# Folding three more adaLN chunks on VectorE in an attention and MLP trunk, with the double steps of two units placed differently

## The reference, cut to what matters

```python
c_act = jax.nn.silu(c)
for i in range(DEPTH):                       # DEPTH = 2
    mod = c_act @ ada_w[i] + ada_b[i]        # ada_w[i]: 2048 x 12288
    sh_mix, sc_mix, g_mix, sh_mlp, sc_mlp, g_mlp = jnp.split(mod, N_MOD, axis=-1)
    h = rmsnorm(x, norm_mix[i]) * (1 + sc_mix) + sh_mix
    mix = fox_mixer(h, ...) if i % 2 == 0 else short_conv_mixer(h, ...)
    x = x + g_mix * mix
    h = rmsnorm(x, norm_mlp[i]) * (1 + sc_mlp) + sh_mlp
    x = x + g_mlp * (jnp.square(jax.nn.relu(h @ w_up[i])) @ w_down[i])
return rmsnorm(x, final_norm)
```

## Time and profile before

| | |
|---|---|
| time, median of 3 runs | 2293.26 us (2293.22 to 2294.5) |
| profiled execution, its own time | 2293.36 us |
| its span | 2291.5 us |
| PE busy | 2251.9 us, 98% |
| DVE busy | 1698.0 us, 74% |
| ACT busy | 1096.8 us, 48% |
| granted PE clock, mean | 0.997 |

### The profile page before, as it was taken

The page is one execution under the profiler, slowest core; times in us unless marked ns, Lnnn a source line. Parts: engine busy times, 40 slices in busy tenths (PEclk is TensorE's granted clock), DMA queues, the critical chain, the costliest instruction groups (busy, mean ns, idle before and its releaser), DMA issues.

```text
span 2291.5 us, 30019 instructions
## 1 busy us (share of the span) xinstructions
PE 2251.9 (98%) x11688; PEld 1919.4 (84%) x11688; DVE 1698.0 (74%) x1642; ACT 1096.8 (48%) x1264; POOL 173.1 (8%) x339
## 2 busy tenths in 40 slices
PE   6999999999999999999999999999999999999998
PEld 5999998878888888888878888887888888888886
DVE  6888999968958957967977888866895555555555
ACT  4355444464445435435545444446443543543553
POOL 0001221101101101101100111100110000000000
PEclk9999999999999999999999999999999999999999
DMA  9987999959968968967966888855986556565563
GB/s 363 386 320 256 347 352 368 349 191 320 340 212 304 348 212 291 336 234 274 328 243 242 305 327 331 319 184 173 320 302 215 184 184 202 184 197 188 184 214 116
DMA packets 271812, 615.71 MB, mean 269 GB/s; under 512 B 15472, under 2 KB 15808, under 8 KB 271296
## 3 DMA queue, kind: packets, MB, share of 16 engines
q1 hardware_dynamic: 220480, 437.56, 55.5%
q0 software_dynamic: 46080, 167.79, 20.1%
q10 hardware_dynamic: 5120, 8.49, 1.1%
HBM read 611.66 MB, written 2.13 MB: 268 GB/s over the span
## 4 chain that ended last, share of the span: by engine, by line
PE 90%; DVE 4%; DMA 2%; issue 2%; ACT 1%; SPq 0%; ACTq 0%; DVEq 0%
PE ps L516 19%; PE ps L517 18%; PE ps L518 18%; PE ps L504 15%; PE ps L505 8%; PE ps L491 2%; PE ps L492 2%; PE ps L493 2%; DMA start_ring<-in_ada_w_dram 2%; DVE hb L1464 1%; DVE acc L1464 1%; DVE square_out L1464 1%; DVE w_lo L1444 0%; PE ps L596 0%; ACT w_hi L916 0%
## 5 line engine op out<-in xcount | busy, mean ns | idle before, releaser
L916 ACT ACTIVATE w_hi<-raw 128x1024 fp32r<-128x1024 f32 x721 | 762.8, 1060 | 965.3 <-PE ps L518 698.3
L1444 DVE TENSOR_TENSOR w_lo<-raw,w_hi 128x1024 fp32r<-128x1024 f32 x721 | 877.3, 1223 | 443.2 <-ACT w_hi L916 441.9
L504 PE MATMUL ps<-h,w_hi 128*128 128x512 f32 x1536 | 541.2, 397 | 0.0
L516 PE MATMUL ps<-w_hi,mid 128*128 128x512 f32 x1280 | 499.8, 390 | 0.2 <-DVE w_lo L1444 0.2
L518 PE MATMUL ps<-w_lo,mid 128*128 128x512 f32 x1280 | 498.2, 389 | 0.0
L517 PE MATMUL ps<-w_hi,mid 128*128 128x512 f32 x1280 | 498.1, 389 | 0.0
L505 PE MATMUL ps<-h,w_lo 128*128 128x256 f32 x1536 | 431.2, 281 | 0.0
L504 PEld LDWEIGHTS ps<-h,w_hi 128*128 128x128 f32 x1536 | 288.4, 188 | 70.5
L516 PE MATMUL ps<-w_hi,h 128*128 128x512 f32 x756 | 298.9, 395 | 4.1 <-DVE w_lo L1444 1.9
L518 PE MATMUL ps<-w_lo,h 128*128 128x512 f32 x756 | 294.6, 390 | 0.0
L517 PE MATMUL ps<-w_hi,h 128*128 128x512 f32 x756 | 294.4, 389 | 0.0
(11 more groups left out here) (246 smaller groups left out, 1801.7 us busy)
## 6 DMA issues: line engine op xcount, KB each, us to landing
ada_raw<-in_ada_w_dram POOLq DMA_DIRECT2D x320, 512.0 KB, 6.4
raw<-in_mlp_w_up_dram SPq DMA_DIRECT2D x128, 1024.0 KB, 5.3
raw<-in_mlp_w_down_dram SPq DMA_DIRECT2D x128, 1024.0 KB, 5.6
raw<-in_fox_w_in_dram SPq DMA_DIRECT2D x48, 1024.0 KB, 11.1
raw<-in_conv_w_in_dram SPq DMA_DIRECT2D x48, 1024.0 KB, 7.5
start_ring<-in_ada_w_dram SPq DMA_DIRECT2D x64, 512.0 KB, 12.1
raw<-in_fox_w_out_dram SPq DMA_DIRECT2D x16, 1024.0 KB, 9.0
raw<-in_conv_w_out_dram SPq DMA_DIRECT2D x16, 1024.0 KB, 5.2
```

The costliest lines, as they stand in the source:

```text
L504: mm(o, hi[:, jc], both, start=(k == 0), stop=False, skip_group_check=True)
L516: mm(o, xh, hi, start=(k == first), stop=False)
L916: op(w_hi[:, e % WR], raw[:, e // 2, EK * (e % 2):EK * (e % 2 + 1)], ACT.Copy).then_inc(hi_ready, 1)
L1444: v.tensor_tensor(w_lo[:, e % WR], raw[:, e // 2, EK * (e % 2):EK * (e % 2 + 1)], w_hi[:, e % WR].bitcast(F32), ALU.subtract).then_inc(spl ...
```

## The change

It has two parts. Chunks 0, 1 and 2 are folded as well (chunk 5 stays as it is). And units 6 and 7 have step tables of their own: both still take 11 steps, but unit 6 takes single steps behind its first three pairs and double steps behind pairs 3, 4 and 6, and unit 7 takes double steps behind pairs 0, 2, 4 and 5 and none behind pair 7.

```diff
-FOLDED = [i for i, (b, _) in enumerate(ADA) if PARTS[b] in GATE or i >= A_MLP0]
+FOLDED = [i for i in range(len(ADA)) if i != A_MLP0 - 1]
...
 ELEVEN = [2, 1, 2, 1, 1, 2, 1, 1]
+RISING = [1, 1, 1, 2, 2, 1, 2, 1]
+FALLING = [2, 1, 2, 1, 2, 2, 1, 0]
...
-PLAN_QKV = plan([NONE] * N_START + [ELEVEN] * 7 + [LATE, DENSE, SEVEN, NONE])
+PLAN_QKV = plan([NONE] * N_START + [ELEVEN, RISING, FALLING] + [ELEVEN] * 4 + [LATE, DENSE, SEVEN, NONE])
```

## The result

| | before | changed |
|---|---|---|
| median | 2293.88 us (4 runs, 2293.22 to 2296.01) | 2308.10 us (4 runs, 2307.72 to 2309.35) |
| ratio | | 1.0063 [1.0051, 1.0075] |
| profiled execution, its span | 2293.36, 2291.5 us | 2307.72, 2305.7 us |
| granted PE clock, mean | 0.997 | 0.994 |

The changed kernel is 14.2 us slower: the sign that was forecast, twice its size (+7.6 us), and outside the range.

The account below looks back on a forecast made before the run. DVE was taken to bound units 6 to 11, making PE wait: 2293.4 + 6.0 (lateness) + 1.6 (lower clock) = 2301.0 us, 0.33% slower. Range 2291 to 2306 us, the main case's own 2297.5 to 2306 us.

Parts of the forecast that it names:

- What bounds the kernel: Units 6 to 9: DVE decides when PE starts the scores of groups 2 and 3; margin at group 2 0.40 us.
- What DVE is given, unit 6 and unit 7: DVE gets 9.1 us more work; reciprocals 1.1 us late, unit 7 adds 3.4 us, scores of group 2 4.1 us later.
- the second sum of unit 6: DVE's work in unit 6 from the split near 245.1 us to the reciprocals at 256.2 us, summed to 11.1 us.
- The saving of chunk 0: PE's 1.57 us from folding chunk 0, forecast to be lost in the wait before the turn of group 1.
- What PE is spared: Folded sums cost PE 0.22 us instead of 1.79 us: 1.57 us spared for a chunk, 4.7 us for three.
- Units 8 to 11: DVE gets 3.6 us more, 1.7 us covered by idle time; scores of group 3 late by 4.1 + 1.9 = 6.0 us.
- The clock: PE's clock falls behind one of two waits, at the scores of groups 2 and 3: 1.6 us, ends 0 and 3.2.
- The rule's reading that both places pay: By the Trainium skill's rule the clock falls behind both waits, making the sum +9.2 us rather than +7.6 us.
- What would show it: Signs: PE waits at groups 1 to 3, DVE windows 97% or more from 253 to 361 us, constant distance from group 3's exponentials.
- DVE has the time and PE keeps its 4.7 us: Rival: the 0.4 us margin holds 3.4 us of new DVE work, giving 2288.7 us; chance 0.12.
- The small-wait case: Rival: 3.0 us wait at the scores of group 2, clock holds, +1 to +4.5 us, about 2296 us; chance 0.16.
- The rival of a longer fall: Clock falls at both places or for longer: 6.0 + 3.2 us or more, 2303 to 2306 us; a third of 0.72.

Follow-up runs that it names:

- e1_fold_only: Kernel before with chunks 0, 1 and 2 folded and its old step tables kept: 2308.48 us, ratio 1.0062.
- e4_fold1_behind: Changed kernel with new tables for units 7 and 8, so that chunk 1 is folded behind `low_attn` of group 1: 2301.95 us, 6.15 us under the changed kernel.
- e6_tables_c: Kernel before with only chunks 0 and 1 folded as well, and its own step tables for units 6 to 12: 2290.72 us, ratio 0.9989.
- e5_tables_a: Kernel before with chunks 0, 1 and 2 folded and new step tables for units 6 to 12, chunk 1's fold behind `low_attn`: 2290.38 us, ratio 0.9987.
- e3_keep_busy: Changed kernel with unused matmuls put into PE's three long waits: 2301.95 us, ratio 1.0031 to the kernel before.
- e2_table_only: Kernel before with the new step tables of units 6 and 7, chunks 0 to 2 not folded: 2296.16 us, ratio 1.0012.
- e8_chunk2_unfolded: Changed kernel, tables included, with chunk 2 not folded: 2305.09 us, 3.0 us under the changed kernel.

## Why the prediction was right in sign and wrong in size

**What bounds the kernel: right.** DVE decides at the scores of groups 2 and 3, and the margin of 0.40 us did not hold the new work. `e1_fold_only` and `e4_fold1_behind` move the wait by moving DVE's work, as that asks.

**What DVE is given, unit 6 and unit 7: right.** 9.0 us of work (9.1 forecast), reciprocals at 256.11 (256.2), turn of group 1 at 259.28 (259.2) after a wait of 1.7 us on ACT, scores of group 2 4.23 us late (4.1). The terms of the second sum of unit 6 add up to 11.0 us and not 11.1 us, which changes nothing. The saving of chunk 0 was lost in that wait, as forecast.

**What PE is spared: the size right, the use as forecast in the changed kernel.** None of the 4.7 us arrives there. In `e6_tables_c`, where PE hardly waits, 2.87 of 3.1 us do. In `e5_tables_a` 0.95 of 4.7 us do at the end of the stage, near the 1.2 us that its waits of 2.2 and 1.3 us leave.

**Units 8 to 11: too small.** The step took 1.7 of the 3.6 us of new DVE work as covered by idle time of DVE, and so added 1.9 us, with 2.9 us as the upper end. Where the clock does not disturb it, in `e3_keep_busy`, the lateness grows from 4.32 to 7.74 us, by 3.4 us. Practically nothing was covered. The idle time of 2.33 us is a wait for `w_hi`, whose ring slot PE frees behind the scores: when the scores are late this wait moves along with them, at 2.85 us. Idle time that follows the late engine is no cover for lateness. It can be filled only by work that the order puts in front of it, as `e5_tables_a` does.

**The clock: the step that failed.** It took 1.6 us, with ends of 0 and 3.2 us. Measured by `e3_keep_busy`, 6.15 us in the medians and 6.5 us at the turn of group 3: 3.1 us behind the scores of group 2 (part of which was absorbed later; the scores of group 3 lie 10.26 - 7.74 = 2.5 us further back) and 4.0 us behind those of group 3. Two errors are in it. Both places paid and not one. And the price for a place came from one stay in the start stage. Windows of 1 us show a granted clock of 0.84 from 71 us, 0.50 from 72 to 75 us and 0.96 from 75 us, so that stay was over in about 3.4 us and 1.6 us was right for it. It was no measure for another place: "more if the level lasts" was written beside it without a number, and in this stage PE worked at the lower level for 6.6 and 8.6 us and lost half of that. Even behind the same one-column matmuls the stay is not fixed: from 70 to 75 us, long before any changed instruction, the granted clock is 0.67 in the kernel before, 1.00 in the changed kernel and 0.50 in `e1_fold_only`, which comes out of this stretch 1.1 us later. With the sum corrected at both steps, by the traces, 4.3 + 3.4 + 6.5 = 14.2 us, the whole is there.

The Trainium skill (TensorE: Matmul & The Clock Gate, "What's actually happening") has activity release the throttle. `e3_keep_busy` agrees: useless matmuls in the gaps kept the granted clock at 1.00 and made the kernel 6.15 us faster. The rule's reading that both places pay was the better one; its +9.2 us was still short, by the length of the stays and by the lateness of units 8 to 11.

**What would show it.** PE did not start the scores of group 2 before 282 us, and from the turn of group 3 the distance of the traces stays within 0.4 us. DVE's idle times of 1.25 and 1.50 us in units 6 and 7 are gone. DVE's windows filled to 98% from 253 to 289 us (35.31 of 36), but only to 90% from 289 to 361 us where 97% was named: a slow PE makes DVE wait in turn, 5.92 us in one place.

**The rivals.** That DVE has the time and PE keeps its 4.7 us was false for this order, and the rule of the Trainium skill beside it (Perfetto Trace Analysis, "Identifying the Most-Contended Engine"), taken over the whole program, pointed the wrong way for this order: the engine of 98% was spared work and the kernel lost 14.2 us. The section does not rank TensorE by the busy share of its matmuls but names the share of its weight loads as one measure, and that is 84%, still above DVE's 74%. `e6_tables_c` shows the part in it that is true: with another order DVE does have the time, and PE keeps 2.87 of 3.1 us. The small-wait case fell with the wait of 3.73 us. The rival of a longer fall was the right one, but its 2303 to 2306 us was too low for the same two reasons, and the range ended with it.

## What to carry to other kernels

Ask of each idle stretch of the engine that you load whether it stands still or moves with the engine that you make late; only the first kind covers anything, and filling the second kind takes an order made for it. Price a new wait of PE twice, once for its length and once for what PE loses behind it at the lower clock, and take the upper end for the whole stay there, since here it was nearly as large as the wait (3.1 us behind 3.73 us, 4.0 us behind 4.9 us in two pieces). When work between two nearly full engines is exchanged, the place of each piece is worth more than its amount: the same folding gave +14.2, +8.5 or -3.4 us, in medians, by the table beside it.

## What the runs showed of the hardware that was not expected

- Among dense matmuls, the waits of PE of 2.47 us and more in these traces (2.47, 2.76, 2.79 and 3.73 us; at the scores of group 3 a shorter wait stood close before) had matmuls at the lower level behind them. Those of up to 1.71 us that stood alone did not (1.71 us at a turn in the changed kernel, 1.36 us in `e2_table_only`, 1.32 us in `e8_chunk2_unfolded`). What lies between was not tried.
- The stay at the lower level is not fixed: behind the same wait of 3.73 us it ended near 291 us in the changed kernel and near 293.6 us in `e8_chunk2_unfolded`. Behind one wait it cost 3 to 4 us of time. At 70 us, with the same instructions ahead of it in all kernels, the clock did not fall in the changed kernel and in `e5_tables_a`, and fell in the other eight traces.
- Unused matmuls made a kernel faster. They cost next to nothing where PE would have waited anyway: the scores of group 2 came 0.09 us later.
- Two stretches of some 100 us, from 838 and from 1929 us, ran 1 to 2 us slower in some executions than in others, with PE busy for over 99% and a granted clock of 1.00, whatever the kernel. The cause is unknown.
